# The causal mask of the prompt scores: from a TensorE product to a VectorE addition

## The chip, the cores and the metric

The kernel runs on one core of one Trainium2 chip. The metric is the device time of one execution in microseconds (us), from the start of the program to its end. The engines are PE (TensorE; PEld is its weight load), DVE (VectorE), ACT (ScalarE), POOL (GpSimd) and SP, which issues most of the DMAs.

## The reference, cut to what matters

One inference step of a two-layer decoder with a prompt of 1,024 tokens and a sample group. The part that the change touches is the prompt's attention (8 heads, 96 wide), in blocks of 128 queries:

```python
sc = jnp.einsum('bqhd,bkhd->bhqk', qi, k).astype(jnp.float32) * MLA_SCALE
sc = jnp.where(pos[None, :] <= pi[:, None], sc, NEG_INF)
p = jax.nn.softmax(sc, axis=-1).astype(c.dtype)
return jnp.einsum('bhqk,bkr->bqhr', p, c)
```

Everything else (projections, gated linear attention, memory attention, the paged attention of the sample group, the output projection) is as it was.

## The kernel before, in words

Each layer first works through eight prompt tiles of 128 tokens (t = 0 to 7) and one sample tile, then through 256 pages for the sample group, then through the output projections. Every engine has one instruction stream written out by hand, and semaphores order them against each other. There is no scheduler: each engine takes its instructions in the order of the code.

At the end of a prompt tile stands a loop over the 8 heads. A head h of tile t passes through these steps:

1. PE, `scores(h)`: the product of the queries with `nk = (t + 1) * 128` keys into PSUM (banks 4 and 5 for even heads, 6 and 7 for odd ones), then one more product of a bf16 identity with the bf16 mask `maskb`, which adds -1e30 above the diagonal of the last 128 columns. Its end is told with `s_ps`.
2. DVE, `maxima(h)`: the row maximum over all nk columns (L1225) and its product with -SCALE (L1226), told with `s_max`.
3. ACT, `probs(h)`: the exponential with the row sum (L793), told with `p_ready`.
4. PE: t + 1 transposes of the probabilities (L1771), told with `pT_ps`.
5. DVE copies up to four of the transposed blocks out of PSUM (L1238); in tiles 4 to 7 ACT copies the rest (L807).
6. PE: the product with the values (L1506), in pairs of heads.

PE runs ahead by two heads: behind the transposes of head h it issues `scores(h + 2)`. In tiles 0 to 3 `scores(0)` and `scores(1)` stand ahead of the gate projection `project(..., O_GMLA, ...)` (16 records at L1512); in tiles 4 to 7 `scores(1)` stands behind the transposes of head 0. In the same loop DVE has four other instructions: the gate's `gate_log` (L1205) at head 2 and `gate_out` (L1209) at head 3, and the evacuation of the next tile's turned input, `turned_x` (L984), at heads 4 and 5. PE turns that input (L1579) behind the transposes of heads 4 and 5, the first half only after `gate_out`, and behind the transposes of head 6 it starts the next tile's first projection, `project_gv(t + 1)` (L1512), which waits for both `turned_x`.

`own(...)` and `tell(...)` make DVE wait for the instruction just issued before it takes the next.

Of the kernel before, what the change touches and what calls it, by code (L numbers as in the profile page):

```python
# [19 lines left out]
ALU = mybir.AluOpType  # L20
# [3 lines left out]
P = 128  # L24
# [69 lines left out]
def build(nc, a, out):  # L94
    ctx = ExitStack()
    with ctx:
        def sb(name, shape, dt=F32):
            return ctx.enter_context(nc.sbuf_tensor(name, shape, dt))
# [11 lines left out]
        ps = ctx.enter_context(nc.psum_tensor("ps", [P, 8, 512], F32))  # L110
# [34 lines left out]
        identb = sb("identb", [P, P], BF16)  # L145
        maskb = sb("maskb", [P, P], BF16)
# [43 lines left out]
        qT = W[0:QK, 0:H * P].rearrange("p (h n) -> p h n", h=H)  # L190
# [10 lines left out]
        kT = region[0:QK, 0:H * SEQ].rearrange("p (h n) -> p h n", h=H)  # L201
# [62 lines left out]
        def chunk(ap, c):  # L264

            return ap.rearrange("p (r c) -> p c r", c=2)[:, c, :]
# [632 lines left out]
        def _(dve):  # L899
            own = Own(dve, s.dve_step)  # L900

            def tell(ins, sem, n):

                ins.then_inc(sem, 1)
                dve.wait_ge(sem, n + 1)

            tt, ts, stt, cp = dve.tensor_tensor, dve.tensor_scalar, dve.scalar_tensor_tensor, dve.tensor_copy

            def heads(ap, h):
                return ap.rearrange("p (h d) -> p h d", h=h)  # L910

            def per_head(ap, T, h, d):

                return ap.unsqueeze(2).to_broadcast([T, h, d])
# [19 lines left out]
            for t in range(2):  # L934
                c = 32 + 12 * t
                dve.wait_ge(s.mkv_ss, t + 1)
                tell(ts(us[:, c:c + 1], st[:, c:c + 1], 1.0 / D, EPS, ALU.mult, ALU.add), s.mean_ready, mem_row(t))
            for t in range(2):
                c = 32 + 12 * t
# [26 lines left out]
            for L in range(DEPTH):  # L966
# [53 lines left out]
                for t in range(NT):  # L1020
# [26 lines left out]
                    else:  # L1047

                        own(dve.memset(mqT, 0.0))
                        for e in range(2):  # L1050
                            w = slice(MD * e, MD * e + MD)
                            for c in range(2):
                                ins = cp(mqT[w, c, :].rearrange("p (b e n) -> p b e n", b=DB, e=2)[:, :, e, :],
                                         ps[w, 6, 256 + c * P:256 + c * P + TS].rearrange("p (b n) -> p b n", b=DB))
# [148 lines left out]
                    def gate_log(i, g_, src):  # L1203
                        dve.wait_ge(s.gates_exp, n_gexp(n) + 2 * i + 1)
                        tell(stt(g_, src, 0.0, g_, ALU.min, ALU.subtract), s.gates_ready, n_gates(n) + 2 * i)  # L1205
# [5 lines left out]
                    if pm_:  # L1211
                        dve.wait_ge(s.mo_ps, m + 1)
                        own(dve.reciprocal(us[:, 44:48], st[:, 48:52]))
                        tell(tt(heads(MO, MH), heads(ps[:, 5, 256:512], MH), per_head(us[:, 44:48], T, MH, MD), ALU.mult), s.mo_ready, m)
                        nk = (t + 1) * P

                        def maxima(h):
                            nh = m * H + h
                            dve.wait_ge(s.s_ps, nh + 1)

                            if nh >= 2:
                                dve.wait_ge(s.p_ready, nh - 1)
                            bank = 4 + 2 * (h % 2)
                            src = ps[:, bank, 0:nk] if nk <= 512 else ps[:, bank:bank + 2, :].rearrange("p c n -> p (c n)")[:, 0:nk]
                            own(dve.tensor_reduce(st[:, 62 + h % 2:63 + h % 2], src, X, ALU.max))  # L1225
                            tell(ts(us[:, 52 + h % 2:53 + h % 2], st[:, 62 + h % 2:63 + h % 2], -SCALE, None, ALU.mult), s.s_max, nh)  # L1226

                        maxima(0)
                        if t < 4:
                            maxima(1)  # L1230
                        gate_log(0, gb, ps[0:T, 7, :])
                        gate_out(0, gb, ps[0:T, 7, :])
                        own(tt(xn[:, 512:1024], xn[:, 512:1024], gb, ALU.mult))
                        for h in range(H):
                            if 0 < h < H - 1:
                                maxima(h + 1)
                            dve.wait_ge(s.pT_ps, m * H + h + 1)
                            tell(cp(ptTs[h % 2][:, 0:min(t + 1, 4), :], ps[:, h % 2 if t < 4 else 0, 0:min(nk, 512)].rearrange("p (j n) -> p j n", n=P)), s.pT_evac_v, m * H + h)  # L1238
                            if h == 0 and t >= 4:
                                maxima(1)  # L1240
                            if h == 2:
                                gate_log(1, ga, gmla)
                            if h == 3:
                                gate_out(1, ga, gmla)
                            if h == 4:
                                turned_x(t + 1, 0)
                            if h == 5:
                                turned_x(t + 1, 1)
                        dve.wait_ge(s.o_ps, m + 1)
                        dve.wait_ge(s.p_ready, m * H + H)  # L1250
                        own(dve.reciprocal(us[:, 54:62], st[:, 52:60]))
                        own(tt(heads(xn[:, 0:512], H), heads(ps[:, 2, :], H), per_head(us[:, 54:62], P, H, VD), ALU.mult))
                        tell(tt(xn[:, 0:512], xn[:, 0:512], gate[:, 0:512], ALU.mult), s.mix_ready, n)
                        continue
# [245 lines left out]
        def _(pe):  # L1500
            mm, tp = pe.matmul, pe.transpose
# [69 lines left out]
            for L in range(DEPTH):  # L1571
# [38 lines left out]
                for t in range(NT):  # L1610
# [22 lines left out]
                    for c in range(2):  # L1633
                        ins = tp(ps[:, 6, 256 + c * P:256 + c * P + T], mq[0:T, c * P:c * P + P], ident[0:T, 0:T])
                    ins.then_inc(s.mqT_ps, 1)
                    if pm_:
# [7 lines left out]
                        for h in range(MH):  # L1644
                            w = slice(MD * (h % 2), MD * (h % 2) + MD)
                            ins = mm(ps[:, 6 + h % 2, NM * (h // 2):NM * (h // 2) + NM], mqT[w, h // 2, :], mkT[w, h // 2, :], start=True, stop=True)
# [11 lines left out]
                    for c in range(2):  # L1658
                        ins = tp(ps[:, 2, c * P:c * P + T], chunk(ck[0:T, 0:R], c), ident[0:T, 0:T])
# [29 lines left out]
                    for c in range(2):  # L1689
                        ins = mm(ps[0:T, 0, :], cT[:, c, 0:T], w_uk[:, c, :], start=c == 0, stop=c == 1)  # L1690
                    ins.then_inc(s.kn_ps, 1)
                    if pm_:
                        pe.wait_ge(s.mp_ready, m + 1)
                        for j in range(8):
                            ins = tp(ps[:, 6 + j // 4, (j % 4) * P:(j % 4) * P + P], pt[:, 0, j * P:j * P + P], ident[:])
# [4 lines left out]
                    for c in range(3):  # L1700
                        ins = tp(ps[:, 3, c * P:c * P + T], cq[0:T, c * P:c * P + P], ident[0:T, 0:T])
# [7 lines left out]
                    for e in range(2):  # L1709
                        for c in range(3):  # L1710
                            ins = mm(ps[0:T, 2 + e, 0:4 * QK], cqT[:, c, 0:T], w_uq[:, c, 4 * QK * e:4 * QK * e + 4 * QK], start=c == 0, stop=c == 2)  # L1711
                    ins.then_inc(s.q_ps, 1)

                    if pm_:
                        if n == 0:
                            pe.wait_ge(s.mkT_evac, 2)
                        for c in range(2):
                            ins = mm(ps[:, 1, :], cT[:, c, :], w_uv[:, c, :], start=c == 0, stop=c == 1)  # L1718
# [4 lines left out]
                        for h in range(MH):  # L1723
                            for c in range(2):
                                ins = halves(ps[:, 5, 256 + MD * h:256 + MD * h + MD], ptT[:, 2 * h + c, :], mv[:, c, MD * h:MD * h + MD], P, c == 0, c == 1)
# [3 lines left out]
                        for h in range(H):  # L1729
                            ins = tp(ps[0:QK, h // 4, (h % 4) * P:(h % 4) * P + P], qk[:, 1, QK * h:QK * h + QK], ident[:])  # L1730
# [3 lines left out]
                        for h in range(H):  # L1734
                            ins = tp(ps[0:QK, 2 + h // 4, (h % 4) * P:(h % 4) * P + P], qk[:, 0, QK * h:QK * h + QK], ident[:])
                        ins.then_inc(s.kqv_ps, 1)
                        project_part(ps[0:T, 7, GW:GW + MW], T, O_GMEM, MW, KD - 2, KD).then_inc(s.gates_ps, 1)
                        nk = (t + 1) * P

                        def scores(h):  # L1740

                            bank = 4 + 2 * (h % 2)
                            for c in range(0, nk, 512):
                                w = min(512, nk - c)
                                last = c + w == nk
                                ins = mm(ps[:, bank + c // 512, 0:w], qT[:, h, :], kT[:, h, c:c + w], start=True, stop=not last)  # L1746
                            ins = mm(ps[:, bank + (nk - P) // 512, (nk - P) % 512:(nk - P) % 512 + P], identb[:], maskb[:], start=False, stop=True)  # L1747
                            ins.then_inc(s.s_ps, 1)

                        pe.wait_ge(s.qT_evac, 2 * m + 1)  # L1750
# [13 lines left out]
                        for h in range(H):  # L1764
# [4 lines left out]
                            for j in range(t + 1):  # L1769
                                b = j // 4 if t >= 4 else h % 2  # L1770
                                ins = tp(ps[:, b, (j % 4) * P:(j % 4) * P + P], pt[:, h % 2, j * P:j * P + P], ident[:])  # L1771
# [17 lines left out]
                            for h_ in {0: (0,), 2: (1, 2), 4: (3, 4), 6: (5, 6), 7: (7,)}.get(h, ()):  # L1789
                                transposed(h_)  # L1790
                                for j in range(t + 1):
                                    ins = halves(ps[:, 2, VD * h_:VD * h_ + VD], ptTs[h_ % 2][:, j, :], vv[:, j, VD * h_:VD * h_ + VD], P, j == 0, j == t)
# [229 lines left out]
                for b in range(DB):  # L2022
                    for c in range(2):
                        o_ = (2 * b + c) * 64
                        ins = mm(ps[:, 6 + o_ // 512, o_ % 512:o_ % 512 + 64], chunk(acc[:, b, 0:R], c), fold[:, 0:64], start=True, stop=True)
# [3 lines left out]
                for h in range(H):  # L2029
                    for c in range(2):  # L2030
                        ins = mm(ps[0:TS, 5, VD * h:VD * h + VD], latT[:, (c * H + h) * TS:(c * H + h) * TS + TS], w_uv[:, c, VD * h:VD * h + VD], start=c == 0, stop=c == 1)
# [11 lines left out]
                for k in range(KD):  # L2043
                    for c in range(2):
                        ins = mm(ps[TS * c:TS * c + TS, 2, :], m_T[p][:, k, 0:TS], w_out[:, k, 512 * c:512 * c + 512], start=k == 0, stop=k == KD - 1)
# [59 lines left out]
```

## Time and profile before

| what | value |
|---|---|
| median of 3 runs | 2792.41 us (2791.17 to 2795.13) |
| the profiled execution, its own time | 2792.35 us |
| span of its instructions | 2790.6 us |
| busy PE / DVE / ACT | 98% / 68% / 32% |
| granted TensorE clock | 0.999 |

The span runs from the first to the last instruction; the time holds 1.75 us more, which lies around it. In the rows below, a record of PE's own duration overlaps its neighbours, since matmuls are pipelined; in the chain that ended last each piece is counted once, so its lengths add up. A number in brackets at the end of a timeline row is how long the engine sat idle before it, and who released it.

### The profile page before, as it was taken

What the parts mean: (1) busy time and instruction counts of PE and PEld (TensorE: products, weight loads), DVE (VectorE), ACT (ScalarE), POOL (GpSimd) and SP (SyncE); (2) the same over time, 40 slices, a digit from 0 to 9 for tenths busy, and PEclk for the clock granted to TensorE, in tenths of its full rate; (3) what the DMA queues carried; (4) which work ended last, traced back from release to release, by engine and by line L of the source; (5) the groups of instructions that cost most, each with busy time, mean ns of one, the idle gap of its engine ahead of it and who ended that gap; (6) DMA issues with size and microseconds to landing.
All of it is one profiled execution on the core that took longest, in us unless ns stands there. A gap on an engine that the chain in (4) does not pass through costs nothing.

```text
span 2790.6 us, 54559 instructions
## 1 busy us (share of the span) xinstructions
PE 2748.2 (98%) x17973; PEld 1619.7 (58%) x17973; DVE 1890.6 (68%) x3801; ACT 880.7 (32%) x1903; POOL 329.6 (12%) x467
## 2 busy tenths in 40 slices
PE   8999999999999999999999999999999999999999
PEld 4666677765455555555466667777545555555553
DVE  3666655567898888886245666566488888888842
ACT  1333333342333333332013333333323333333300
POOL 0111100002111111110010000001021111111100
PEclk9999999999999999999999999999999999999999
DMA  7222223325444444544532222233353444445422
GB/s 289 73 65 68 70 72 74 75 65 175 113 111 128 130 114 128 174 132 136 210 123 60 64 70 68 72 75 72 98 162 103 126 123 130 119 136 183 118 100 87
DMA packets 528940, 313.70 MB, mean 112 GB/s; under 512 B 360009, under 2 KB 512146, under 8 KB 525586
## 3 DMA queue, kind: packets, MB, share of 16 engines
q1 hardware_dynamic: 526912, 309.41, 38.6%
q8 instruction: 143, 2.34, 0.4%
q14 instruction: 139, 1.14, 0.1%
q10 hardware_dynamic: 1746, 0.81, 0.1%
HBM read 287.63 MB, written 89.60 MB: 135 GB/s over the span
## 4 chain that ended last, share of the span: by engine, by line
PE 86%; DVE 9%; ACT 2%; issue 1%; DMA 0%; POOL 0%; SPq 0%; DVEq 0%; ACTq 0%
PE ps L1918 29%; PE ps L1512 13%; PE ps L1997 8%; PE ps L1937 4%; PE ps L1746 4%; PE ps L1949 4%; PE ps L1506 3%; PE ps L1711 3%; PE ps L1771 2%; PE ps L1518 2%; PE ps L1523 2%; PE ps L1931 1%; ACT U L730 1%; PE ps L1718 1%; DVE w_in L1396 1%
## 5 line engine op out<-in xcount | busy, mean ns | idle before, releaser
L875 ACT ACTIVATE w_in<-ps 128x512 f32<-128x512 f32 x512 | 305.7, 597 | 688.1 <-PE ps L1918 629.4
L1918 PE MATMUL ps<-w_uk,region 128*128 128x512 f32 x1040 | 470.2, 596 | 0.0
L1396 DVE TENSOR_REDUCE w_in<-w_in 128x8 f32<-128x512 f32 x512 | 351.2, 686 | 48.8 <-ACT w_in L875 32.7
L1512 PE MATMUL ps<-w_in,xT 128*128 128x256 f32 (+6 forms) x1360 | 378.3, 431 | 2.2 <-DMA w_in<-in_w_in 1.6
L1918 PEld LDWEIGHTS ps<-w_uk,region 128*128 128x128 f32 x1040 | 187.0, 190 | 216.5 <-issue 216.2
L1512 PEld LDWEIGHTS ps<-w_in,xT 128*128 128x128 f32 (+1 forms) x1360 | 246.4, 185 | 113.1 <-issue 69.3
L1918 PE MATMUL ps<-w_uk,xT 128*128 128x512 f32 x672 | 304.4, 596 | 0.0
L604 POOL TENSOR_TENSOR rs<-us,mhalf 128x1 f32<-128x1 f32 (+4 forms) x132 | 130.9, 991 | 1331.2 <-DVE us L1034 729.0
L1918 PEld LDWEIGHTS ps<-w_uk,xT 128*128 128x128 f32 x672 | 120.7, 190 | 136.8 <-issue 135.9
L1918 PE MATMUL ps<-w_uk,W 128*128 128x512 f32 x336 | 151.8, 593 | 1.0 <-ACT w_in L875 1.0
L1746 PE MATMUL ps<-region,W 96*128 96x512 f32 (+3 forms) x384 | 146.8, 494 | 0.1
L1225 DVE TENSOR_REDUCE st<-ps 128x1 f32<-128x256 f32 (+7 forms) x128 | 97.0, 758 | 68.1 <-PE ps L1747 64.3
L1518 PE MATMUL ps<-w_in,xT 128*128 128x256 f32 (+1 forms) x496 | 142.9, 431 | 0.0
L653 POOL TENSOR_TENSOR xt<-region,mkv 128x128 f32<-128x128 f32 x64 | 29.2, 457 | 912.4 <-issue 901.6
L793 ACT ACTIVATE U<-ps,us 128x256 f32<-128x256 f32 (+7 forms) x128 | 94.8, 740 | 120.0 <-DVE us L1226 85.9
L1997 PE MATMUL ps<-region,glw 128*128 128x512 f32 x256 | 113.1, 595 | 0.0
L1997 PE MATMUL ps<-region,xT 128*128 128x512 f32 x256 | 112.3, 594 | 0.0
L1518 PEld LDWEIGHTS ps<-w_in,xT 128*128 128x128 f32 x496 | 89.4, 190 | 28.8
L1238 DVE COPY ws<-ps 128x512 f32<-128x512 f32 (+3 forms) x64 | 37.8, 591 | 97.6 <-PE ps L1771 96.6
L1918 PEld LDWEIGHTS ps<-w_uk,W 128*128 128x128 f32 x336 | 60.4, 190 | 66.4 <-issue 66.4
L1771 PE MATMUL ps<-ident,U 128*128 128x128 f32 x576 | 88.7, 281 | 7.0 <-ACT U L793 6.3
L1018 DVE STREAM_TRANSPOSE region<-region 128x512 f32<-128x512 f32 x82 | 91.4, 1114 | 3.1 <-DVE w_in L1406 0.3
(403 smaller groups left out, 4048.4 us busy)
## 6 DMA issues: line engine op xcount, KB each, us to landing
pages_by_quarter<-in_cache_ckv SPq DMA_DIRECT2D x512, 128.0 KB
region<-pages_by_quarter SPq DMA_DIRECT2D x80, 512.0 KB, 4.0
region<-in_cache_ckv SPq DMA_DIRECT2D x320, 128.0 KB, 2.2
w_in<-pages_by_quarter SPq DMA_DIRECT2D x48, 512.0 KB, 4.0
w_in<-in_cache_ckv SPq DMA_DIRECT2D x192, 128.0 KB, 2.1
w_in<-in_w_in SPq DMA_DIRECT2D x16, 1240.0 KB, 11.1
mix_quarters<-xn SPq DMA_DIRECT2D x16, 512.0 KB, 3.2
region<-in_cache_kpe SPq DMA_DIRECT2D x512, 16.0 KB
```

Source lines behind the costliest of these rows:

```text
L604: pool.tensor_tensor(rs[0:T, c:c + k], us[0:T, c:c + k], mhalf[0:T, 0:k], ALU.pow).then_inc(s.root_ready, 1)
L875: tell(act.activation(sqb[j % 4], ps[:, j if k == 0 and j < 2 else 2 + j % 2, :], ACT.Square), s.pkn_sq, np_)
L1225: own(dve.tensor_reduce(st[:, 62 + h % 2:63 + h % 2], src, X, ALU.max))
L1396: tell(dve.tensor_reduce(pst[:, 0, j * H:j * H + H], heads(sqb[j % 4], H), X, ALU.add), s.pkn_red, np_)
L1512: ins = mm(out, xT[:, k, 0:T], w_in[:, k, c0:c0 + w], start=k == 0, stop=k == KD - 1)
L1518: ins = mm(out, xT[:, k, 0:T], w_in[:, k, c0:c0 + w], start=k == 0, stop=k == KD - 1)
L1746: ins = mm(ps[:, bank + c // 512, 0:w], qT[:, h, :], kT[:, h, c:c + w], start=True, stop=not last)
L1771: ins = tp(ps[:, b, (j % 4) * P:(j % 4) * P + P], pt[:, h % 2, j * P:j * P + P], ident[:])
L1918: ins = mm(ps[:, key_bank(k, j), :], page[:, o_:o_ + P], w_uk[:, c, :], start=c == 0, stop=c == 1)
L1937: ins = mm(ps[half:half + 64, j // 4, so_:so_ + 64], page[:, o_:o_ + 64], qt[:, c, 64 * b:64 * b + 64], start=False, stop=c == 1 and j % 4 ...
L1949: ins = mm(ps[e:e + 64, 6, 0:RW], psb[:, k % 2, 64 * i:64 * i + 64], pages_of(k)[:, i, :], start=i < 2, stop=i >= G - 2)
L1997: ins = mm(ps[:, 2 + c, :], m_T[p][:, k, :], w_out[:, k, 512 * c:512 * c + 512], start=k == 0, stop=k == KD - 1)
```

## The change

The product of identity and mask is taken out of `scores(h)`, for all 8 heads, 8 tiles and 2 layers (128 products). In `maxima(h)` DVE now adds `maskb` to the last 128 columns of the scores, in place in PSUM, ahead of the maximum (128 additions). The score matmuls stop their accumulation themselves.

```diff
@@ maxima(h), DVE
                             src = ps[:, bank, 0:nk] if nk <= 512 else ps[:, bank:bank + 2, :].rearrange("p c n -> p (c n)")[:, 0:nk]
+                            own(tt(src[:, nk - P:nk], src[:, nk - P:nk], maskb[:], ALU.add))
                             own(dve.tensor_reduce(st[:, 62 + h % 2:63 + h % 2], src, X, ALU.max))
@@ scores(h), PE
                                 w = min(512, nk - c)
-                                last = c + w == nk
-                                ins = mm(ps[:, bank + c // 512, 0:w], qT[:, h, :], kT[:, h, c:c + w], start=True, stop=not last)
-                            ins = mm(ps[:, bank + (nk - P) // 512, (nk - P) % 512:(nk - P) % 512 + P], identb[:], maskb[:], start=False, stop=True)
+                                ins = mm(ps[:, bank + c // 512, 0:w], qT[:, h, :], kT[:, h, c:c + w], start=True, stop=True)
                             ins.then_inc(s.s_ps, 1)
```

On DVE, in the head loop of a prompt tile (here tile 0 of the first layer, heads 2 to 5), the order was: the copies of turned probabilities (L1238, into `U` or `ws`), the two instructions of `maxima` (L1225, L1226) for the head after, and one of the four other instructions.

```order
L1238 COPY U<-ps 128x128
L1205 SCALAR_TENSOR_TENSOR gate<-ps,gate 128x512
L1225 TENSOR_REDUCE st<-ps 128x1
L1226 TENSOR_SCALAR us<-st 128x1
L1238 COPY ws<-ps 128x128
L1209 TENSOR_TENSOR gate<-gate,ps 128x512
L1225 TENSOR_REDUCE st<-ps 128x1
L1226 TENSOR_SCALAR us<-st 128x1
L1238 COPY U<-ps 128x128
L984 TENSOR_TENSOR xT<-ps,gains 128x512
```

The same piece of the changed kernel, where the lines from L1225 on are numbered one higher and L1225 is the addition:

```order
L1239 COPY U<-ps 128x128
L1205 SCALAR_TENSOR_TENSOR gate<-ps,gate 128x512
L1225 TENSOR_TENSOR ps<-ps,maskb 128x128
L1226 TENSOR_REDUCE st<-ps 128x1
L1227 TENSOR_SCALAR us<-st 128x1
L1239 COPY ws<-ps 128x128
L1209 TENSOR_TENSOR gate<-gate,ps 128x512
L1225 TENSOR_TENSOR ps<-ps,maskb 128x128
L1226 TENSOR_REDUCE st<-ps 128x1
L1227 TENSOR_SCALAR us<-st 128x1
L1239 COPY U<-ps 128x128
L984 TENSOR_TENSOR xT<-ps,gains 128x512
```

One instruction more stands ahead of each maximum, and with it ahead of each copy, gate instruction and `turned_x` that follows; nothing else of DVE's order moved.

On PE, the same stretch of tile 0 from the transposes of head 2 (L1771) to those of head 4, before, with the score product at L1746, the mask product at L1747 and the value products at L1506:

```order
L1771 MATMUL ps<-ident,U 128x128
L1746 MATMUL ps<-region,W 128x128
L1747 MATMUL ps<-maskb,identb 128x128
L1506 MATMUL ps<-region,ws 64x64 x2
L1506 MATMUL ps<-region,U 64x64 x2
L1771 MATMUL ps<-ident,U 128x128
L1746 MATMUL ps<-region,W 128x128
L1747 MATMUL ps<-maskb,identb 128x128
L1771 MATMUL ps<-ident,U 128x128
```

And in the changed kernel:

```order
L1770 MATMUL ps<-ident,U 128x128
L1746 MATMUL ps<-region,W 128x128
L1507 MATMUL ps<-region,ws 64x64 x2
L1507 MATMUL ps<-region,U 64x64 x2
L1770 MATMUL ps<-ident,U 128x128
L1746 MATMUL ps<-region,W 128x128
L1770 MATMUL ps<-ident,U 128x128
```

The mask product is gone from behind each score product, and the rest stands in its old order.

## Rows read from the trace of the kernel before

**Rows 1.** The page, part 1: busy time, share of the span, instructions.

```profile
PE 2748.2 (98%) x17973; PEld 1619.7 (58%) x17973; DVE 1890.6 (68%) x3801; ACT 880.7 (32%) x1903; POOL 329.6 (12%) x467
```

**Rows 2.** The mask product's line: records, shortest, median and longest ns.

```profile
L1747 PE MATMUL ps<-maskb,identb x128: 220/221/222, 97.4 to 1987.7; 128*128 128x128 bf16 x128
```

**Rows 3.** The chain that ended last, tile 7: start, length in us, what.

```profile
604.70 1.72 PE ps L1746 x4
606.41 0.06 PE ps L1747
606.47 2.05 PE ps L1506 x64
608.52 1.02 PE ps L1771 x8
```

**Rows 4.** The chain that ended last, end of tile 1's head loop.

```profile
171.35 0.43 DVE st L1225
171.79 0.02 issue
171.81 0.17 DVE us L1226
...
176.11 0.70 DVE xT L984
...
176.86 1.18 PE ps L1512 x4
```

**Rows 5.** Timeline of DVE, the copy of head 1 in tiles 0 to 3.

```profile
106.41 0.29 DVE L1238 COPY ws<-ps 128x128 f32<-128x128 f32 x1 [0.24 <-PE ps L1771]
169.04 0.42 DVE L1238 COPY ws<-ps 128x256 f32<-128x256 f32 x1 [0.32 <-PE ps L1771]
233.69 0.56 DVE L1238 COPY ws<-ps 128x384 f32<-128x384 f32 x1 [0.33 <-PE ps L1771]
300.96 0.69 DVE L1238 COPY ws<-ps 128x512 f32<-128x512 f32 x1 [0.34 <-PE ps L1771]
```

**Rows 6.** Timeline of DVE, later copies in tile 0 (heads 2, 3).

```profile
107.48 0.29 DVE L1238 COPY U<-ps 128x128 f32<-128x128 f32 x1 [0.27 <-PE ps L1771]
109.30 0.29 DVE L1238 COPY ws<-ps 128x128 f32<-128x128 f32 x1 [0.29 <-DVE us L1226]
```

**Rows 7.** Timeline of tile 3, the last `turned_x`.

```profile
310.69 0.69 DVE L984 TENSOR_TENSOR xT<-ps,gains 128x512 f32<-128x512 f32 x1
```

**Rows 8.** The chain that ended last, tile 3, the next tile's projection.

```profile
311.66 3.48 PE ps L1512 x15
```

**Rows 9.** Timeline, exponential and transposes of head 1 in tiles 4 and 7.

```profile
370.23 0.19 ACT L793 ACTIVATION_READ_ACCUMULATOR U<-ps,us 128x1 f32 x1
370.47 0.77 PE L1771 MATMUL ps<-ident,U 128*128 128x128 f32 x5 [0.20 <-ACT U L793]
...
600.70 0.19 ACT L793 ACTIVATION_READ_ACCUMULATOR U<-ps,us 128x1 f32 x1
...
600.95 1.09 PE L1771 MATMUL ps<-ident,U 128*128 128x128 f32 x8
```

**Rows 10.** DVE's groups by shape: busy us, mean ns, idle us before.

```profile
L1038 DVE TENSOR_TENSOR ws<-ps,rs 128x256 f32<-128x256 f32 x16 | 6.8, 425 | 0.6
L1096 DVE TENSOR_TENSOR W<-ps,W 128x128 f32<-128x128 f32 x16 | 4.7, 292 | 0.6
L925 DVE TENSOR_TENSOR W<-ws,sinn 128x128 f32<-128x128 f32 x16 | 4.7, 292 | 0.6
L925 DVE TENSOR_TENSOR rk<-rkey,sinn 128x16 f32<-128x16 f32 x16 | 2.8, 174 | 0.5
```

**Rows 11.** The core's span and mean granted clock.

```profile
core 0: 2790.6 us, clock 0.999
```

**Rows 12.** Timeline of PE, transposes of head 4 in tile 0.

```profile
109.77 0.33 PE L1771 MATMUL ps<-ident,U 128*128 128x128 f32 x1 [0.96 <-ACT U L793]
```

## The prediction

> **What bounds the kernel now.** The page's first part says PE: it is busy for 2748 of 2791 us, DVE for 68% and ACT for 32% [rows 1]. Taken alone, that would make any product taken off PE a gain and any instruction added to DVE free. But a share is a mean over stages, so the second view is the chain that ended last, read tile by tile through the head loops, because only those hold the change. There are two kinds of loop. In tile 7 PE follows PE without a break: scores, mask product, value products, transposes [rows 3]. In tile 1 the chain runs through DVE: maximum, scaling, copy, gate instruction, and so on until the second `turned_x` ends at 176.81, and PE's next projection starts 0.05 us later [rows 4]. The reader should see that PE waits there although the page calls it 98% busy: with one to three blocks of keys PE has little to do per head, while DVE's four instructions of 512 columns cost 0.70 us each whatever the tile. The third view is the timeline, for DVE's idle stretches: what is idle there can take up an addition, the rest cannot. No other stage is touched; the 256 pages and the output projections keep their instructions.
>
> **What the change removes.** 128 mask products. A record lasts 221 ns [rows 2], but it overlaps its neighbours; in the chain it takes 0.06 us [rows 3], and that is what PE gets back where it is the bound. If PE were the bound in every head, that would be 128 x 0.06 = 7.7 us. The scores are also told to DVE 0.06 us earlier.
>
> **What it adds.** 128 additions on DVE, 128 x 128, one operand in PSUM, one in SBUF, result in PSUM. The trace has no DVE instruction that writes PSUM, nor one with a bf16 mask, so the price has bounds. The nearest row is the product of 128 x 128 with one operand in PSUM: 0.292 us, the same as with both in SBUF [rows 10]; so reading PSUM costs nothing visible and I take the write to cost nothing either. To it comes the 0.02 to 0.03 us between two DVE instructions [rows 4]. I take 0.32 us per addition. Below it, 0.174 us is what the smallest such product takes [rows 10]; above it, 0.425 us for 256 columns [rows 10], as if the write in place were a second pass.
>
> The Trainium skill, "VectorE: DVE Perf Modes", section on the TRN2 errata, gives a PSUM source a larger fixed term (120 cycles) than an SBUF source (58 cycles). The trace does not agree: both sources take 292 ns [rows 10]. By the page's PSUM figure the addition would be an estimated 0.26 us, and the sum below about 1 us smaller.
>
> **Tiles 0 to 3, where DVE is or becomes the chain.** The additions of heads 0 and 1 lie ahead of the gate projection and are hidden under it (16 records of 512 columns, during which DVE waits). From head 2 on, DVE's stream is: maximum 2, copy 1, maximum 3, copy 2, gate, maximum 4, copy 3, gate, maximum 5, copy 4, `turned_x`, maximum 6, copy 5, `turned_x`; then PE's next projection. Five additions fall into it, 5 x 0.32 = 1.60 us.
> - The addition of head 2 meets the idle stretch ahead of the copy of head 1: 0.24, 0.32, 0.33 and 0.34 us in tiles 0 to 3 [rows 5], of which some 0.03 is the ordinary gap. It takes up all of it but 0.1 us in tile 0.
> - The four others, 1.28 us, meet almost none. In tile 0 there are two stretches, 0.27 and 0.29 us long [rows 6], that give back 0.24 and 0.26; in the second layer I expect only the first. In tile 1 there is none [rows 4]. In tile 2 DVE's stream ended right when PE began, and about 0.15 is absorbed by the earlier scores and by short waits. In tile 3 the last `turned_x` ended at 311.38 [rows 7] and PE began at 311.66 [rows 8], so 0.24 is slack, and short waits take some 0.2 more.
> - PE saves one mask product (0.06) ahead of the gate projection, two in tile 3.
>
> So tile 0 loses 0.8 us (1.1 in the second layer), tile 1 1.25, tile 2 1.05, tile 3 0.7.
>
> What stands behind the late instruction: ACT's exponentials of heads 4 to 6 start up to 0.8 us later and PE's transposes with them, but they end before `turned_x` does, so they add nothing more. Where PE started the projection late, the value products of heads 5 to 7 come behind it as before, and the mask products saved in between are lost in PE's waits.
>
> **Tiles 4 to 7, where PE is the chain.** Here `scores(1)` comes late, and the chain passes once through DVE and ACT: maximum 1, exponential 1, transposes 1. In tile 4 PE waited 0.20 us for ACT [rows 9]; in tile 7 the accumulator read ended at 600.89 and the transposes started at 600.95 [rows 9], no slack either. So the addition of head 1 costs 0.32 - 0.06 = 0.26 us in each of the four. Afterwards PE saves up to five masks (0.30) and the one of head 0 (0.06), if DVE and ACT keep up. Following each head with the durations of the timeline, they don't quite in the short tiles: ACT's copy of head h stands behind its exponential h + 1, and that waits for the maximum, now up to 0.8 us later; the value products of heads 2 and 4 wait for that copy. I get +0.35 us for tile 4, +0.2 for tile 5, +0.1 for tile 6 and 0 for tile 7. The bounds of this part are -0.48 (eight masks saved) and about +0.6 per tile.
>
> **The sum.** First layer 0.8 + 1.25 + 1.05 + 0.7 + 0.35 + 0.2 + 0.1 = 4.45 us, second layer 0.3 more, 4.75: together 9.2 us. The profiled execution took 2792.35 us, as good as the median of the runs, 2792.41; with the sum, 2801.6 us, 0.33% more. About 39 additions lie on the path (tiles 0 to 3 some 15 a layer, 4 to 7 four to five). At 0.174 us instead of 0.292 each, the sum is 4.6 us smaller (2797.0); at 0.425 it is 5.2 us larger (2806.8).
>
> **The rivals.**
> 1. *Slack takes most of it.* Only tiles 0 and 1 pay (about 2.2 us a layer), and in the other six PE keeps 0.06 x 8 = 0.48 each: 4.4 - 5.8 = -1.4 us, 2791.0. For it: DVE is idle in 32% of the span [rows 1]. Against it: in tiles 2 and 3 the stream of DVE ends at most 0.28 us ahead of PE [rows 7, 8], and five additions are 1.6 us. Chance 0.15.
> 2. *PE's gain arrives in full*, the forecast's opposite: 2792.4 - 7.7 = 2784.7. Its place is every head, its price the 0.06 us of rows 3; it would need the additions to be hidden everywhere. Rows 4 speak against it: it decides only if an addition costs less than DVE's waits, some 0.03 us in tile 1. Chance 0.06.
> 3. *The write to PSUM is dear*: an addition of 0.425 us or more, 2807. Nothing shows it; nothing in the trace excludes it. Chance 0.14.
> 4. *PE's waits lower its clock.* The granted clock is 0.999 [rows 11], that is 2.4 GHz, although PE already waits up to 0.96 us at a time in tile 0 [rows 12]; the changed kernel has such waits of about 1.5 us, in four tiles a layer. If the clock fell to 1.2 GHz behind each, a projection of 3.48 us [rows 8] would take as much again: 8 x 3.5 = 28 us on top, about 2830. Chance 0.02. The Trainium skill, "TensorE: Matmul & The Clock Gate", Part 1, says that an idle array falls to half rate; it is the rule that speaks against this change. For the waits of before the trace shows no such fall; for longer ones it shows nothing.
>
> **How the numbers follow.** The likeliest case, the sum, has a chance of 0.63 and its own range 2798 to 2805. A difference under 0.2% (5.6 us, 2786.8 to 2798.0) is about what a measurement of this kernel can't tell from no change. Rivals 3 and 4 are slower, rival 1 is the same, rival 2 is faster, and of the likeliest case a twentieth lies under 2798. Faster 0.06, same 0.19, slower 0.75. The range 2794 to 2808 holds the likeliest case, nearly all of rival 3 and a part of rival 1, about 8 in 10.
>
> **What would show it.** DVE should have 128 additions of about 0.29 us, and the chain in tiles 2 and 3 should run through DVE to the second `turned_x`, as tile 1's did. From the start of the gate projection to the start of `project_gv(t + 1)`, tile 1's stretch should be 1.3 us longer and tile 7's almost the same. The stages outside the prompt's head loops should keep their lengths. The prediction is wrong if the additions last 0.17 or 0.42 us, if the tiles 2 and 3 lose nothing, or if the granted clock falls.

## The result and the profile after

The changed kernel took 2809.4 us (2808.0 to 2810.0, 5 runs) against 2792.7 us (2791.2 to 2795.1): a ratio of 1.006, 95% interval 1.0049 to 1.007. It is slower, as forecast, but by 16.8 us where 9.2 were predicted, and outside the range.

The page's first part of the changed kernel, which answers to [rows 1]:

```profile
PE 2756.3 (98%) x17845; PEld 1619.0 (58%) x17845; DVE 1929.8 (69%) x3929; ACT 880.7 (31%) x1903; POOL 329.6 (12%) x467
```

PE has 128 records less and yet 8 us more of busy time; DVE has the 128 additions. The shares say nothing of a loss. The addition's line, with shortest, median and longest ns:

```profile
L1225 DVE TENSOR_TENSOR ps<-ps,maskb x128: 299/299/300, 98.6 to 2005.2; 128x128 f32<-128x128 f32 x128
```

It lasts 299 ns, 7 more than the row it was taken from [rows 10], and 0.33 us with the gap to the next. So the write into PSUM and the bf16 operand cost 7 ns together beside that row. (By the PSUM figure of the Trainium skill, "VectorE: DVE Perf Modes", section on the TRN2 errata, it was an estimated 0.26 us; the chip took 0.30.)

The chain that ended last, tile 2 of the first layer (start, length in us, what):

```profile
244.57 0.31 DVE ps L1225
244.88 0.02 issue
244.91 0.57 DVE st L1226
...
246.28 0.70 DVE xT L984
246.98 0.02 issue
247.00 0.31 DVE ps L1225
247.31 0.02 issue
247.33 0.57 DVE st L1226
```

Tile 2 now runs through DVE as only tiles 0 and 1 did before; tile 3 does so too. And what the prediction did not expect stands in the clock. The granted clock of the core, which answers to [rows 11], and the chain behind tile 0's head loop:

```profile
core 0: 2808.2 us, clock 0.995
```

```profile
114.03 0.87 PE ps L1580 x4
...
114.99 0.70 DVE xT L984
115.69 0.04 issue
115.74 6.04 PE ps L1513 x16
121.78 0.38 PE ps L1507 x8
```

Before, the same 16 records (there at L1512) took 3.93 us:

```profile
112.76 0.70 DVE xT L984
113.46 0.04 issue
113.50 3.93 PE ps L1512 x16
```

The reader should see the same instructions, with nobody waiting between them, 2.11 us longer. The windows name the cause. Columns: window, its length, busy us of PE, PEld, DVE, ACT and POOL with their counts, granted clock, DMA share, GB/s. Before:

```profile
98.00:112.00 14.00, 12.04 (x64) 6.47 (x62) 8.07 (x24) 7.38 (x20) 0.00 (x0) 1.00 0.29 67
112.00:126.00 14.00, 13.73 (x88) 11.48 (x89) 5.36 (x16) 1.30 (x5) 1.01 (x1) 1.00 0.35 90
1481.00:1495.00 14.00, 13.76 (x87) 11.39 (x86) 5.40 (x15) 1.00 (x5) 1.01 (x1) 1.00 0.15 47
```

The changed kernel, at the same times. Its second layer begins 8.7 us later, so the last row lies inside tile 0's head loop, where the one of before lies behind it:

```profile
98.00:112.00 14.00, 11.61 (x49) 6.29 (x49) 8.87 (x26) 7.78 (x19) 0.00 (x0) 0.92 0.28 64
112.00:126.00 14.00, 13.79 (x66) 10.68 (x64) 4.24 (x14) 1.40 (x7) 0.00 (x0) 0.71 0.29 66
1481.00:1495.00 14.00, 11.40 (x57) 7.77 (x56) 9.27 (x29) 5.23 (x16) 0.00 (x0) 0.78 0.11 26
```

A granted clock of 0.71 over 14 us is a mixture of its two levels, 2.4 and 1.2 GHz. It fell at the end of tile 0 in both layers. This is not a trait of the one profiled execution: the mean granted clock was 0.994 or 0.995 in each of the five, while 67 executions of the kernel before, in the groups below, had 0.997 to 1.000.

**Where the 17.6 us of span are.** The next tile's 32 records of `project_T` take 3.77 us in every tile and serve as a mark; the distance between two marks is one tile. Before, tile 2 ended at the second of these rows, and tile 3 would begin there (first layer, chain that ended last):

```profile
185.61 3.77 PE ps L1523 x32
...
252.00 3.77 PE ps L1523 x32
```

And in the changed kernel:

```profile
191.23 3.77 PE ps L1524 x32
...
258.67 3.77 PE ps L1524 x32
```

Tile 2 went from 66.39 to 67.44 us, 1.05 more. Read in the same way, what each tile costs more, in us:

| tile | predicted | first layer | second layer |
|---|---|---|---|
| 1 | 1.25 | 1.27 | 1.25 |
| 2 | 1.05 | 1.05 | 1.06 |
| 3 | 0.7 | 0.96 | 0.99 |
| 4 | 0.35 | 0.72 | 0.72 |
| 5 | 0.2 | 0.31 | 0.62 |
| 6 | 0.1 | 0.36 | 0.43 |
| 7 | 0 | 0.26 | 0.26 |
| sum | 3.65 | 4.93 | 5.33 |

(Tile 5 took the same in both layers afterwards, 76.5 us; before, it was 0.3 shorter in the second.) That is 10.3 us. Tile 0 accounts for most of the rest: its first mark comes 4.35 us late, of which 0.84 were there before its head loop began, 1.40 arose in the loop and 2.11 in the projection behind it; in the second layer tile 0 costs 3.16. Up to there the kernels differ only in two mask products less, so the 0.84 isn't the change's own work: the granted clock was 0.83 between 60 and 70 us here, and 0.89 between 70 and 80 before. Outside the prompt -0.57 and +0.40 remain.

### The profile page after: what moved, and what is told of

It reads as the page before. It is cut to its first block, busy times and chain, and to the rows that moved or that the text cites. A ratio compares the mean times of both kernels' runs of the same rounds, so it can differ in the third digit from the quotient of the medians.

```text
span 2808.2 us, 54431 instructions
## 1 busy us (share of the span) xinstructions
PE 2756.3 (98%) x17845; PEld 1619.0 (58%) x17845; DVE 1929.8 (69%) x3929; ACT 880.7 (31%) x1903; POOL 329.6 (12%) x467
## 4 chain that ended last, share of the span: by engine, by line
PE 85%; DVE 11%; ACT 2%; issue 2%; DMA 0%; POOL 0%; SPq 0%; DVEq 0%; ACTq 0%
PE ps L1917 30%; PE ps L1513 13%; PE ps L1996 8%; PE ps L1936 4%; PE ps L1948 4%; PE ps L1746 3%; PE ps L1507 3%; PE ps L1712 2%; PE ps L1524 2%; PE ps L1519 2%; PE ps L1770 2%; PE ps L1930 1%; DVE st L1226 1%; ACT U L730 1%; PE ps L1719 1%
## 5 line engine op out<-in xcount | busy, mean ns | idle before, releaser
L1746 PE MATMUL ps<-region,W 96*128 96x512 f32 (+3 forms) x384 | 146.2, 495 | 0.2
L1770 PE MATMUL ps<-ident,U 128*128 128x128 f32 x576 | 89.7, 283 | 17.8 <-ACT U L793 16.8
L1226 DVE TENSOR_REDUCE st<-ps 128x1 f32<-128x256 f32 (+7 forms) x128 | 97.0, 758 | 4.5
```

## The experiments

All but the ones that say otherwise put the mask where two functions tell, on PE by `by_pe(t, h)` and on DVE by `by_dve(t, h)`:

```diff
+                            if by_dve(t, h):
+                                own(tt(src[:, nk - P:nk], src[:, nk - P:nk], maskb[:], ALU.add))
...
-                                ins = mm(..., start=True, stop=not last)
-                            ins = mm(..., identb[:], maskb[:], start=False, stop=True)
+                                ins = mm(..., start=True, stop=not (last and by_pe(t, h)))
+                            if by_pe(t, h):
+                                ins = mm(..., identb[:], maskb[:], start=False, stop=True)
```

Before is `by_pe` always and `by_dve` never, the changed kernel the reverse. Times below are medians against the kernel before on the same chip, which took 2792.9, 2793.2 and 2792.7 us in the three groups.

### Is it tile 0?

```diff
+def by_pe(t, h):
+    return t == 0
+def by_dve(t, h):
+    return t > 0
```

> Additions on VectorE in tiles 1 to 7, the mask product back on PE in tile 0 of both layers. In the changed kernel's trace, tiles 1 to 7 cost 4.9 and 5.3 us more than before and tile 0 the rest, part of it at half TensorE clock. Theory A (the additions of tile 0 lengthen PE's waits there, and the clock falls because of them): no half-clock stretch around the end of tile 0, time 10 us over before, about 2803. Rival B (the clock's fall is not tied to tile 0's additions): the half-clock stretches stay, time 14 us over before, about 2806.5.

2802.6 us (2801.7 to 2807.5), ratio 1.0039 (1.0025 to 1.0052): 9.7 over before, as theory A had it. Tiles 1 to 7 cost what they cost in the changed kernel, but for 0.34 us more in tile 2 of the second layer. Tile 0 is as before in the second layer (+0.01), while in the first one short fall of the clock is still seen (the projection took 4.59 us). Theory A had expected none. The same short fall stands in the first layer of the last two kernels below, which also leave tile 0 as it was (projection 4.59 and 4.58 us, loops 15.74 instead of 15.28), and in the second layer of none. So the trace of the kernel before, without any fall there, is the better case of an untouched tile 0: it stands near an edge even with its products. The executions scatter upwards by 5 us.

### Tile 0 alone

```diff
+def by_pe(t, h):
+    return t > 0
+def by_dve(t, h):
+    return t == 0
```

> The reverse: additions on VectorE in tile 0 alone, mask products in tiles 1 to 7. Theory A: tile 0 pays about 1.3 us a layer in its chain and 2 us more at half clock, 6 to 7 us over before, about 2799. Rival B: the chain's 1.3 us a layer alone, 2.6 us over before, about 2795, clock as before.

2795.2 us (2794.7 to 2797.2), ratio 1.001 (1.0001 to 1.0019): 2.3 over before, which is rival B's number. But the trace shows theory A's mechanism: the projection behind tile 0 took 6.06 us in the first layer, 3.93 in the second, and the loops 16.67 and 16.46 us (before 15.28 and 15.02). The span is only 2.8 us over that of before because this execution reached tile 0's loop 1.0 us earlier and was 1.6 us quicker between the layers, as most of the others were. There the chain of before holds a wait for weights, ahead of the second layer's first projection, and that of this run holds no transfer:

```profile
1412.60 8.24 DMA w_in<-in_w_in
...
1420.88 7.39 PE ps L1512 x32
```

So time and trace point different ways, and this run alone decides nothing.

### No mask at all

```diff
+def by_pe(t, h):
+    return False
+def by_dve(t, h):
+    return False
```

> Neither mask products nor additions (the causal mask of the prompt is left out). What PE gets back alone: theory A, 0.06 us a head in tiles 2 to 7 and little in tiles 0 and 1, where VectorE leads: 6 us under before, about 2786.5. Rival C (a mask product costs PE more than its 0.06 us in the chain, weight loads included): 10 us or more under before.

2791.9 us, ratio 0.9998 (0.9989 to 1.0007): 1.0 us under before, neither of the two. Tiles 1 to 7 gave back 0.10, 0.27, 0.32, 0.26, 0.37, 0.39 and 0.40 us, 2.1 a layer, so 0.05 us a head where PE leads. But tile 0's loop took 16.1 us in both layers instead of 15.3 and 15.0, with nothing added and eight products taken away. From the end of the gate projection to the end of the loop the granted clock was 0.81 in both layers, and over the whole execution it was 0.995 to 0.997 in all eleven. That made a new theory necessary: it is the work taken off PE that costs the clock.

### Filling PE's waits

```diff
-                            for c in range(0, nk, 512):
+                            for c in list(range(0, nk, 512)) * (2 if t == 0 else 1):
```

> The changed kernel, with each score product of tile 0 issued twice (the same values written again), so PE works where it waited. Theory A (PE's waits in tile 0 pull its clock down): the half-clock stretches around the end of tile 0 vanish and with them 4 us: about 2805.5, although PE does more. Rival B (the fall has another cause): the stretches stay, the time is that of the changed kernel, 2809.5, or somewhat over.

2805.6 us (ratio 1.0046, 1.0032 to 1.006), 12.6 over before and so 4.1 less than the changed kernel's 16.8, although PE does more. In the first layer the loop took 16.29 us and the projection 3.93: with the clock up, DVE's chain costs 1.01 us in tile 0. In the second layer the clock still fell once inside the loop (16.94).

### Work taken away, or waits added?

```diff
+def by_pe(t, h):
+    return t > 0
+def by_dve(t, h):
+    return False
```

> Tile 0 of both layers without mask product and without additions (its causal mask is left out), mask products in tiles 1 to 7. Theory D (what pulls the clock down in tile 0 is the work that PE no longer has there): the clock falls around tile 0's head loop without any addition, as in the run without masks, and the time is 1 to 3 us over before although nothing was added. Theory A in its first form (the longer waits behind the additions pull it down): no fall beyond those of before, time within 0.5 us of before.

2796.7 us (2794.1 to 2798.1): 3.4 us over before, ratio 1.001 (1.0001 to 1.002). A kernel that only left out 16 small products became slower. Its windows show why, with a clock under 1.00 in both layers:

```profile
98.00:112.00 14.00, 12.07 (x56) 7.04 (x56) 7.92 (x22) 6.67 (x20) 0.00 (x0) 0.86 0.29 66
112.00:126.00 14.00, 13.79 (x84) 11.45 (x83) 4.69 (x13) 1.03 (x5) 0.34 (x1) 0.89 0.30 74
1467.00:1481.00 14.00, 12.20 (x58) 7.30 (x57) 8.11 (x22) 6.91 (x20) 0.00 (x0) 0.85 0.21 48
1481.00:1495.00 14.00, 13.79 (x85) 11.45 (x84) 4.49 (x12) 0.84 (x3) 0.57 (x1) 0.90 0.08 26
```

The second layer is the sharper evidence, since no untouched tile 0 fell there. And all ten executions had a mean clock of 0.995 to 0.997, against 0.997 to 0.999 of before on this chip.

The reverse keeps the product in tile 0 and adds on DVE as well:

```diff
+def by_pe(t, h):
+    return True
+def by_dve(t, h):
+    return t == 0
```

> Tile 0 with the mask product on PE and the addition on VectorE (the mask is added twice), mask products alone in tiles 1 to 7. Theory D: PE keeps its work, the clock falls less often than in the run with additions alone; tile 0's loops are 1.0 and 1.1 us longer by VectorE's chain, about 2 us over before. Theory A in its first form: half-clock stretches as in the changed kernel (10 and 7 us), 5 to 6 us over before.

2796.2 us (2795.2 to 2797.4), 3.0 over before, ratio 1.001 (1.0 to 1.002), between the two expectations. The projection behind tile 0 took 5.82 us in the first layer, and in the second the clock was 0.83 in the later part of the loop, so here too it fell. Both halves of the change can pull it down: the work taken away and the waits added. Over whole executions the second half shows less: 0.997 or 0.998 in all ten.

### The additions alone

```diff
+def by_pe(t, h):
+    return True
+def by_dve(t, h):
+    return True
```

> Mask product and addition in all tiles (the mask is added twice): the price of the additions alone. From the traces so far, the additions with the products gone cost 5.0 and 5.3 us a layer in tiles 1 to 7, and the products gone alone give back 2.1 a layer. If the two are independent, tiles 1 to 7 cost 7.1 and 7.4 here and tile 0 some 1.1 each: 17 us over before, 2809.5, as slow as the changed kernel. If what PE gets back is lost in its waits once VectorE leads (rival), tiles 1 to 7 cost 5 to 6 a layer: 13 over, 2806.

2810.7 us, 17.4 over before, ratio 1.006 (1.0043 to 1.0077). Tiles 1 to 7 cost 1.40, 1.33, 1.27, 1.04, 0.60, 0.72 and 0.69 us in the first layer, 7.05 in all (7.39 in the second). With what the missing products give back (2.1) that makes 4.9, the changed kernel's number: the two are independent, tile by tile to within 0.1 us. The clock fell here too, though every product was kept: the projections behind tile 0 took 5.97 and 4.97 us.

### The clock kept up

```diff
-                            for c in range(0, nk, 512):
+                            for c in list(range(0, nk, 512)) * (3 if t == 0 else 1):
```

> The changed kernel with each score product of tile 0 issued three times. Theory E (TensorE's clock falls in tile 0 where PE works for too small a share of the loop, through work taken away and through waits added alike): no half-clock stretch at either tile 0, so tile 0 costs only VectorE's chain, 1.0 and 1.1 us, and the whole about 12.5 us over before, 2805.5. Rival B (the fall is not tied to PE's work there): 10 and 7 us at half clock as in the changed kernel, 2809.5 or more.

2805.1 us (ratio 1.0046, 1.003 to 1.0061), 12.5 over before, as theory E had it. Tile 0's loops took 16.55 and 16.54 us, 1.27 and 1.52 over before where 1.0 and 1.1 were expected, so the filling itself may cost some tenths. The granted clock stays up in tile 0 of both layers:

```profile
98.00:112.00 14.00, 12.73 (x69) 7.91 (x67) 8.98 (x27) 6.65 (x18) 0.00 (x0) 1.00 0.29 65
112.00:126.00 14.00, 13.79 (x95) 11.33 (x94) 6.46 (x19) 1.55 (x7) 0.00 (x0) 1.00 0.28 65
1481.00:1495.00 14.00, 12.84 (x89) 10.31 (x90) 7.93 (x24) 3.44 (x12) 0.00 (x0) 1.00 0.03 7
```

And the same filling (twice) without any mask:

```diff
+def by_pe(t, h):
+    return False
+def by_dve(t, h):
+    return False
...
-                            for c in range(0, nk, 512):
+                            for c in list(range(0, nk, 512)) * (2 if t == 0 else 1):
```

> Neither mask product nor addition in any tile (the causal mask is left out), each score product of tile 0 issued twice. Theory E: with the clock kept up in tile 0, what the removal of the products is worth shows at last: 2.1 us a layer in tiles 1 to 7, about 4.2 us under before, 2789. Rival B: as in the run without masks, 1 us under before, 2792.

2787.3 us, ratio 0.9983 (0.9974 to 0.9993): 5.4 under before, where the run without filling had 1.0. The projection behind tile 0 took 3.93 us in both layers. Each layer's eight or sixteen products more in tile 0 thus take 4.1 and 4.3 us off the changed kernel, and eight take 4.4 off the one without masks. The mean clock of the filled kernels' executions is 0.998 or 0.999 in these last two runs, as before.

### The rest of tile 4

In the changed kernel's chain of tile 7, the addition is passed twice, the second time by way of ACT's exponential of head 3 and its copy of head 2 behind it, for which the value products wait:

```profile
607.04 0.31 DVE ps L1225
...
613.03 0.31 DVE ps L1225
...
615.88 0.20 ACT U L793
616.08 0.02 issue
616.10 0.59 ACT U L807
616.70 0.14 issue
616.83 1.15 PE ps L1507 x32
```

The test moves that copy ahead of the exponential:

```diff
-                            if 0 < h < H - 1:
+                            if 0 < h < H - 1 and not (t >= 4 and h > 1):
                                 probs(h + 1)
                             if t >= 4:
...
+                            if 1 < h < H - 1 and t >= 4:
+                                probs(h + 1)
```

> The changed kernel, with ACT's copy of head h ahead of its exponential of head h + 1 for h = 2 to 6 in tiles 4 to 7. If the rest of tile 4's loss is PE waiting for that copy (0.18 us ahead of the value products of head 2 and 0.25 us ahead of the transposes of head 4 in the changed kernel's trace), tile 4's loop falls from 25.03 to 24.7 us or less. Rival (the exponential behind it is the later one): it stays at 25.0 or grows.

Tile 4 cost 0.24 us instead of 0.72 in the first layer and 0.23 in the second, tile 5 0.05 instead of 0.31 (0.37 for 0.62), tiles 6 and 7 stayed within 0.1. So the queue behind ACT's later exponential is shown for tiles 4 and 5. In tile 7 the second addition also left the chain, but in its place PE waits once for the copy and the exponential behind it:

```profile
617.07 0.60 ACT ws L817
617.67 0.02 issue
617.69 1.22 ACT U L803 x2
618.90 0.04 issue
618.95 1.09 PE ps L1786 x8
```

So the test doesn't tell for tiles 6 and 7. This one execution took 2807.4 us.

### A version that might beat both

```diff
+def by_pe(t, h):
+    return not (t >= 5 and h >= 4)
+def by_dve(t, h):
+    return t >= 5 and h >= 4
```

> A version that may beat both: the addition only where the chain ran through PE with VectorE behind it, heads 4 to 7 of tiles 5 to 7 (24 of 128), the mask product everywhere else. By the chain each product there is worth 0.05 to 0.06 us and no addition lies on the path: 1.2 us under before, 2791.5, clock as before; the trace's tile lengths must show it, the time hardly can. Rival: ACT's copies behind the later exponentials take it back, tiles 5 to 7 as long as before or longer.

2793.4 us, ratio 1.0003 (0.9994 to 1.0012), no difference that can be told. Tiles 6 and 7 became 0.09 and 0.18 us shorter in the first layer, tile 5 0.19 longer.

```diff
+def by_pe(t, h):
+    return not (t >= 4 and h >= 3)
+def by_dve(t, h):
+    return t >= 4 and h >= 3
...
-                            if 0 < h < H - 1:
+                            if 0 < h < H - 1 and not (t >= 4 and h > 1):
                                 probs(h + 1)
...
+                            if 1 < h < H - 1 and t >= 4:
+                                probs(h + 1)
```

> As the run before, but additions for heads 3 to 7 of tiles 4 to 7 (40 of 128) and ACT's copy of head h ahead of its exponential of head h + 1 for h = 2 to 6 there. In the changed kernel that order took 0.5 us off tile 4. Expected: 0.2 to 0.25 us off each of tiles 4 to 7, 1.9 us under before, 2791. Rival: in tile 4 VectorE, with 2.9 us of work a head, leads again, and tile 4 is longer than before.

2794.2 us, ratio 1.0004 (0.9995 to 1.0013). In the first layer tiles 6 and 7 became 0.17 and 0.13 us longer and tile 5 0.13 shorter; in the second tile 4 became 0.62 longer, tiles 5 to 7 0.18, 0.17 and 0.34. Expected were four shorter tiles: a miss. No version faster than the kernel before was found.

## Why the prediction was right or wrong

**What bounds each tile** was read rightly: DVE in tiles 0 and 1, then also in 2 and 3, PE with one pass through DVE and ACT from tile 4 on. So was the direction.

**The addition's price** was right to 0.01 us (0.33 on the path against 0.32). Rival 3, a dear write to PSUM, fell with that row.

**What PE gets back** was 0.05 us a head instead of 0.06, and nothing in tile 0; the bound of 7.7 us for rival 2 would have been 4.3 with the clock up by the tiles' sums, 5.4 in time.

**Tiles 1 to 3** came out at 3.3 us a layer against 3.0. **Tiles 4 to 7** are a term of the sum that was mis-sized: 1.65 and 2.03 us a layer against 0.65. The second pass through the chain, by ACT's copy behind its exponential, had been seen, but was counted too low: head 1's 0.26 less six saved products makes -0.10, so the forecast's tiles leave 0.45, 0.30, 0.20 and 0.10 us for it. With the product kept, the additions cost 1.04, 0.60, 0.72 and 0.69 us; less one addition (0.33), the rest is 0.71, 0.27, 0.39 and 0.36, in tile 7 a second whole addition. (What a tile gets back was put at 0.42 there and measured 0.26 to 0.40, the other part of the miss.) That the copy's place is the reason is shown for tiles 4 and 5; for 6 and 7 it is read from the chain alone. Over both layers tiles 4 to 7 make 2.4 us of the miss and tile 3 0.6, together 3.0.

**The step that failed** is rival 4. It was given a chance of 0.02, with a price of 28 us for eight places, on the ground that the clock had stood at 0.999 although PE already waited. In the runs the clock did fall, in tile 0 of both layers and for part of the projection only. Filling PE's waits takes 4.3 us off the time, which is its price. I had asked only whether the waits grow; the windows, and the run that only left the products out of tile 0, show that the work taken away counts as well. The same piece of tile 0 in the first layer, from the end of the gate projection to the end of the loop, shows it in records. In this order: before; the changed kernel; only the products left out; the scores three times; and one of the later kernels that leave tile 0 as it was:

```profile
105.16:113.50 8.34, 6.12 (x53) 4.02 (x52) 6.75 (x21) 4.78 (x14) 0.00 (x0) 1.00 0.30 67
105.93:115.74 9.81, 7.33 (x49) 5.34 (x47) 8.24 (x26) 4.77 (x14) 0.00 (x0) 0.70 0.29 66
104.01:113.50 9.49, 7.35 (x47) 5.32 (x46) 6.75 (x21) 4.78 (x14) 0.00 (x0) 0.72 0.30 68
105.03:114.71 9.68, 8.21 (x73) 6.53 (x71) 8.25 (x26) 4.78 (x14) 0.00 (x0) 1.00 0.30 68
106.33:115.13 8.80, 6.71 (x53) 4.68 (x53) 6.75 (x21) 4.78 (x14) 0.00 (x0) 0.88 0.29 66
```

PE's busy time doesn't order them: where the clock is low each record lasts longer, so fewer records look busier (7.35 us for 47 against 6.12 for 53). The Trainium skill, "TensorE: Matmul & The Clock Gate", Part 1, ties the clock to how busy the array has been; by that rule the products taken off PE count as much as waits do. The run that only left them out agrees, with its clock of 0.72 in this piece. I had weighed its sentence on idle stretches alone.

One reading of the trace was wrong as well. "For the waits of before the trace shows no such fall" rested on the mean of 0.999, and a mean hides a short stretch: the same trace had a fall where PE was busy for 6.42 of 10 us, ahead of tile 0's loop.

```profile
70.00:80.00 10.00, 6.42 (x33) 4.32 (x32) 7.83 (x23) 1.68 (x4) 2.59 (x3) 0.89 0.17 55
```

Together: 9.2 predicted, 3.0 for the mis-sized tiles and 4.3 for the clock make 16.5 of the 16.8 us. The 4.3 is what filling gives back, a little less than the fall's price if the filling costs something. Without the clock's part the time would have lain inside the range.

**Left open.** In single traces the clock also falls elsewhere, in kernels with and without additions: between 60 and 90 us (before too, 0.89 between 70 and 80), between 680 and 720 (0.96 in the changed kernel), and between 2050 and 2080 (0.83 between 2070 and 2080 in the changed kernel). Nothing was changed there, and why it happens in one trace and not in the next was not settled. Nor was it settled in full why the change in tile 0 alone costs 2.3 us, and 7 us when it is made in the other tiles too (2809.4 against 2802.6). In part the traces tell: with tile 0 alone the projection behind it was slow in the first layer only (6.06 and 3.93 us), in the changed kernel in both (6.04 and 5.86), and both partial runs were 1.5 us or so quicker between the layers than before, which counts twice when their differences are added.

## What to carry to other kernels

Read the chain per stage, not the shares: an engine at 98% busy can be the one that waits, and an instruction put on one that is 68% busy lands on the path in every stage where that one leads. On such a chain count an addition once for each way the chain comes back to it, other engines' queues included. And before taking small work off TensorE in a stage where it waits, look at the granted clock there: the work may be free and yet hold the clock up.

## What the runs showed of the hardware

- Taking the mask products out of tile 0, with nothing put in their place, made the kernel 3.4 us slower; the granted clock in the loop went from 1.00 to 0.86 and 0.85 in the two layers, and that of whole executions from 0.998 to 0.996 in the mean. Repeating products that write the same values again, in PE's waits, made two kernels 4 us faster.
- A VectorE addition in place in PSUM, 128 x 128 with a bf16 operand in SBUF, takes 299 ns, against 292 ns for a product from PSUM into SBUF.
- A 128 x 128 bf16 product with its own weights costs 0.05 us between fp32 matmuls where PE leads (tiles 6 and 7 became 0.39 and 0.40 us shorter for eight), though its record lasts 221 ns.
- Where PE waits, a tile with the same instructions can lose clock in one trace and not in another: an untouched tile 0 of the first layer had 1.00 in one trace and 0.88 in three.
